# Behind three post-norms: the old residual's share of the first tile is multiplied early, and the feed of the first projection is reordered

## The chip, the cores and the metric

The kernel runs on one core of a Trainium2 chip. The metric is the device time of one execution in microseconds (us). Before the change it is 1817.71 us, the median of 3 runs that lay between 1817.23 and 1820.11 us.

## What is computed

The reference is a stack of transformer-like layers in fp32 on a 1024-wide residual `x` of 512 positions. The part that matters here is the seam between two sub-layers:

```python
x = x + rms_norm(y, norm_mix_post)      # post-norm of a sub-layer's output y
h = rms_norm(x, norm_mem_pre)           # pre-norm of the next sub-layer
q = h @ w_mq                            # its first projection
```

This happens three times with a post-norm: behind the mixer (in front of the memory attention, `w_mq`), behind the memory attention (in front of the MLP, `w_up`), and behind the MLP (in front of the first projection of the second block, `ab_w_in`). Where the root of the pre-norm enters only as a factor for each position, the kernel multiplies with the not yet normed `x * gain` and scales the product afterwards.

## The kernel before

Everything is kept transposed: a tile is 128 features (partitions) by 512 positions, and `X` holds 8 such tiles. Every operand of a matmul is split into a high part in the reduced fp32 format and a low part that holds the rest, so that each product of a weight tile and an activation tile takes three matmuls of 128x128 by 128x512: high times high, high times low, low times high. `AH` and `AL` hold high and low of `x * gain`, `WH` and `WL` those of the weights (four slots; POOL splits each loaded weight unit with two instructions, L315 and L320, as soon as TensorE has done with the slot). The names of the three seams are the pair of the sub-layer that ends and the one that begins: `o1` and `m2`, `o2` and `m3`, `m3` and `b`.

At a seam the engines do this, each in its program's order, held together by semaphores:

- TensorE ends the last output units. `post_stat` adds up the squares of `y` over the partitions with a product with ones (L494, and L496 for the last tile), then `quad` computes four output tiles (banks 0 to 3) at once, one k-tile after the other: for k-tile 0 eight matmuls with `AH` (L439, L440) and four with `AL` (L443), for each further k-tile twelve in groups of three (L454, L455, L456). `stat` (L485) multiplies the sum of squares of the new `x` with ones. Behind `m3` and `b` further units of 24 matmuls follow (L406 to L408); `m2` has none, there the attention follows (L748).
- ScalarE (ACT) squares `y` and scales it by the gain (L1404, L1405; L1443, L1445 behind the MLP), forms the root (Ln L1159, Exp L1161), and then for each tile of the new `x` writes the high part (L1174) and the square (L1177), the squares into two PSUM banks in turn. At the end it forms the root of the pre-norm (L1159, L1161 again).
- VectorE (DVE) in `x_update` does for each tile: `y` times root into a PSUM bank (`scaled`, L1981), `X += ` that (L1991), the low part `x * gain - high` (`low`, L1662), and the addition of a square (`add_square`, L1985). The low part has both its tensor inputs in SBUF. In `m2` the reads of the four banks (L1685) follow, in `m3` a clearing of `Y` (L2039) and the MLP's own work on squares (L2044, L2048).

The order on VectorE is the one written out in the code, one tile ahead:

```python
for t in range(KT):
    done(v.tensor_tensor(X[:, t, :], X[:, t, :], o, ALU.add)...)
    if t >= 2: add_square(t - 1)
    if t < KT - 1: n = scaled(t + 1)
    low(q, t, gain)
add_square(KT - 1)
```

Of the kernel before, what the change touches and what calls it, by code (L numbers as in the profile page):

```python
# [57 lines left out]
def each(stages, kind, n):  # L58
# [41 lines left out]
    "ah": each(["m1", "mm", "m2", "m3", "b", "f0", "c", "f1"], "ah", 8),  # L100
# [5 lines left out]
    "al": each(["m1", "mm", "m2", "m3", "b", "f0", "c", "f1"], "al", 8),  # L106
# [59 lines left out]
UPM = [0, 1, 2, 3, 4, 5, 0, 1]  # L166
POST_T = {"m2": 4, "m3": 4, "b": 6}
# [4 lines left out]
def build(nc, xT, memT, wstream, vecs, w_f, w_gk, gk_up, pool_w, bands, ident_d, masks_bf, gla_masks, out):  # L172
    ctx = ExitStack()
    with ctx:
# [219 lines left out]
        def _(pe):  # L394
            mm = nc.tensor.matmul

            def unit(bank, h, l, n=None, slot=None, split=None, ready=None):
# [5 lines left out]
                for k in range(KT):  # L403
                    if ready:
                        ready(k)
                    mm(bank, WH[:, slot, k, :], h(k), start=(k == 0), stop=False)  # L406
                    mm(bank, WH[:, slot, k, :], l(k), start=False, stop=False)  # L407
                    last = mm(bank, WL[:, slot, k, :], h(k), start=False, stop=(k == KT - 1))  # L408
                last.then_inc(sem("unit_done"), 1)

# [81 lines left out]
            def post_stat(p):  # L492
                pe.wait_ge(sem(f"{p}_ysum"), nth(f"{p}_ysum", 7))
                mm(B[7][:], ONES[:], SUM, start=True, stop=False)  # L494
                pe.wait_ge(sem(f"{p}_ysq"), nth(f"{p}_ysq", 8))
                mm(B[7][:], ONES[:], TMP[:, 5, :], start=False, stop=True).then_inc(sem(f"{p}_ystat"), 1)  # L496

# [244 lines left out]
            post_stat("o1")  # L742
            quad(U0["mq"], B[0:4], a_high, a_low, "mq_quad", tiles_ready("m2_al"), None, tiles_ready("m2_ah"), lambda: stat("m2"))
# [24 lines left out]
            post_stat("o2")  # L768
# [14 lines left out]
            def mlp(p, name, before=None, up=UP0, xbanks=(0, 1, 2, 3, 4, 5), tail=False):  # L783
# [3 lines left out]
                def chunk(i, first, halved=False):  # L787
                    q0 = U0[name] // 4
                    if first:
                        quad(U0[name], [B[b] for b in up[0:4]], a_high, a_low, f"{p}_quad", tiles_ready(f"{p}_al"),  # L790
                             bank_read if before else None, tiles_ready(f"{p}_ah") if p == "m3" else None)
                        stat(p)
                        for j in range(4, KT):
                            if up[j] in up[:j]:
                                pe.wait_ge(sem(f"{p}_relu"), nth(f"{p}_relu", up.index(up[j]) + 1))
                            unit(B[up[j]][:], a_high, a_low, n=U0[name] + j)
# [31 lines left out]
            post_stat("m3")  # L828
            quad(U0["bq"], B[0:4], a_high, a_low, "bq_quad", tiles_ready("b_al"), None, tiles_ready("b_ah"))
            stat("b", cols=True)  # L830
            for n in range(4, 8):
                if n >= 6:
                    pe.wait_ge(sem("b_bq_read"), nth("b_bq_read", n - 5))
                unit(B[n % 6][:], a_high, a_low, n=U0["bq"] + n)
# [317 lines left out]
        def _(act):  # L1152
# [254 lines left out]

            y_out("o1", U0["out"], "mix_post",
# [4 lines left out]
            attention("mem")  # L1413
            y_out("o2", U0["mo"], "mem_post",
# [4 lines left out]
            def mlp(p, name, post=None, banks=UP0):  # L1419
# [17 lines left out]
                if post:  # L1437
                    for t in range(KT):
# [208 lines left out]
        def _(dve):  # L1647
# [11 lines left out]

            def low(p, t, gain):  # L1660
                dve.wait_ge(sem(f"{p}_ah"), nth(f"{p}_ah", t + 1))
# [314 lines left out]
            def x_update(p, q, gain):  # L1976
# [6 lines left out]
                def add_square(t):  # L1983
                    dve.wait_ge(sem(f"{q}_xsq"), nth(f"{q}_xsq", t + 1))
                    own(v.tensor_tensor(SUM, SUM, B[POST_SQ[q][t % 2]][:], ALU.add).then_inc(sem(f"{q}_sum"), 1), f"{q}_sum")  # L1985

                dve.wait_ge(sem(f"{p}y_rb"), nth(f"{p}y_rb", 1))
                n = scaled(0)
                for t in range(KT):
                    dve.wait_ge(sem("dve_step"), nth("dve_step", n))  # L1990
                    done(v.tensor_tensor(X[:, t, :], X[:, t, :], o, ALU.add).then_inc(sem(f"{p}_x"), 1), f"{p}_x")  # L1991
                    if t >= 2:
                        add_square(t - 1)
                    if t < KT - 1:
                        dve.wait_ge(sem(f"{p}_x"), nth(f"{p}_x", t + 1))
                        n = scaled(t + 1)
                    low(q, t, gain)
                add_square(KT - 1)

            y_sum("o1")  # L2000
# [6 lines left out]
            split_out("mem", 3, 0)  # L2007
            y_sum("o2")
# [29 lines left out]
            def mlp(p, name, q=None, gain=None, post=False, tail=False):  # L2038
# [24 lines left out]
                up(i)  # L2063
                for j in range(KT - 2 if tail else KT):
# [387 lines left out]
```

## Time and profile before

| what | value |
|---|---|
| median of 3 runs | 1817.71 us |
| the profiled execution: its own time | 1819.97 us |
| the profiled execution: its span | 1818.2 us |
| mean granted TensorE clock | 0.994 |
| busy: PE / weight load / DVE / ACT / POOL | 98% / 79% / 56% / 25% / 59% |

The span runs from the first instruction to the last; the execution's own time lies 1.8 us above it. All times in the rows below are counted from the start of the span. A matmul's listed duration includes its passage through the array, so that successive matmuls overlap in the listing; what one costs is the distance from one start to the next. The same holds, to a smaller degree, for ACT and DVE.

### The profile page before, as it was taken

How to read it: one execution, taken by the hardware profiler on the slowest of the kernel's cores; microseconds unless marked ns; L12 is line 12 of the kernel's file. 1: busy time of each engine (PE TensorE's matmuls, PEld its weight loads, DVE VectorE, ACT ScalarE, POOL GpSimd, SP SyncE). 2: the span in 40 equal slices, each digit the busy share in tenths (PEclk: the TensorE clock that was granted, in tenths of full speed). 3: DMA queues.
4: the chain of work that ended last, by engine and by line, in shares of the span. 5: the costliest groups of instructions: out<-in, count | busy, mean ns of one | idle time of the engine just before them, and what ended most of it. 6: DMA issues, size and time to landing. Idle time of an engine off the chain costs nothing.

```text
span 1818.2 us, 22611 instructions
## 1 busy us (share of the span) xinstructions
PE 1775.4 (98%) x8364; PEld 1437.0 (79%) x8364; DVE 1026.7 (56%) x1194; ACT 463.4 (25%) x931; POOL 1074.8 (59%) x604
## 2 busy tenths in 40 slices
PE   9998999999999998999999999999999999999997
PEld 7775677788888886767888888887887888888886
DVE  5989465744352576175635252696766562616177
ACT  5427335401010123153201010212335320202011
POOL 7593453566666665434666666675344566666672
PEclk9999999999999999999999999999999999999999
DMA  6231221233223333211333323322221233333331
GB/s 240 68 96 58 74 80 45 82 94 102 94 93 103 93 93 104 82 47 53 98 93 95 103 92 95 102 93 81 69 71 59 81 93 95 102 93 94 102 93 47
DMA packets 46591, 161.44 MB, mean 89 GB/s; under 512 B 5232, under 2 KB 7792, under 8 KB 46384
## 3 DMA queue, kind: packets, MB, share of 16 engines
q1 hardware_dynamic: 45088, 157.31, 28.3%
q10 hardware_dynamic: 1424, 3.02, 0.5%
q8 instruction: 57, 0.93, 0.2%
q14 instruction: 22, 0.18, 0.0%
HBM read 158.21 MB, written 2.10 MB: 88 GB/s over the span
## 4 chain that ended last, share of the span: by engine, by line
PE 92%; DVE 4%; ACT 2%; issue 2%; POOL 1%; DMA 0%; DVEq 0%; POOLq 0%; ACTq 0%
PE bank L406 21%; PE bank L407 21%; PE bank L408 21%; PE bank L454 3%; PE bank L455 3%; PE bank L456 3%; PE bank L474 1%; PE bank L475 1%; PE bank L476 1%; PE bank L1002 1%; PE bank L1038 1%; PE bank L1004 1%; PE bank L1003 1%; DVE bank L1773 1%; PE bank L1053 1%
## 5 line engine op out<-in xcount | busy, mean ns | idle before, releaser
L320 POOL TENSOR_TENSOR WL<-RAW,WH 128x1024 fp32r<-128x1024 f32 x291 | 740.8, 2546 | 24.3
L315 POOL TENSOR_SCALAR WH<-RAW 128x1024 fp32r<-128x1024 f32 x291 | 313.2, 1076 | 674.7 <-PE bank L408 363.7
L406 PE MATMUL bank<-AH,WH 128*128 128x512 f32 x848 | 332.6, 392 | 0.0
L408 PE MATMUL bank<-AH,WL 128*128 128x512 f32 x848 | 330.0, 389 | 0.0
L407 PE MATMUL bank<-AL,WH 128*128 128x512 f32 x848 | 330.0, 389 | 0.0
L406 PE MATMUL bank<-HH,WH 128*128 128x512 f32 x832 | 325.2, 391 | 0.0
L407 PE MATMUL bank<-HL,WH 128*128 128x512 f32 x832 | 324.0, 389 | 0.0
L408 PE MATMUL bank<-HH,WL 128*128 128x512 f32 x832 | 323.7, 389 | 0.0
L1428 ACT ACTIVATE TMP<-bank 128x512 f32<-128x512 f32 x96 | 57.3, 596 | 777.0 <-PE bank L408 739.2
L2048 DVE TENSOR_TENSOR HL<-TMP,HH 128x512 fp32r<-128x512 f32 x96 | 239.1, 2491 | 4.0 <-ACT HH L1433 0.7
L2054 DVE TENSOR_TENSOR Y<-Y,bank 128x512 f32<-128x512 f32 x72 | 49.5, 688 | 309.3 <-PE bank L408 309.3
L2044 DVE TENSOR_TENSOR TMP<-TMP 128x512 f32<-128x512 f32 x96 | 113.0, 1177 | 174.5 <-ACT TMP L1428 174.5
L406 PEld LDWEIGHTS bank<-AH,WH 128*128 128x128 f32 x848 | 159.2, 188 | 36.8 <-issue 4.0
L407 PEld LDWEIGHTS bank<-AL,WH 128*128 128x128 f32 x848 | 159.2, 188 | 33.9 <-issue 1.2
L408 PEld LDWEIGHTS bank<-AH,WL 128*128 128x128 f32 x848 | 159.2, 188 | 33.2
L406 PEld LDWEIGHTS bank<-HH,WH 128*128 128x128 f32 x832 | 156.2, 188 | 36.1 <-DVE HL L2048 3.7
L408 PEld LDWEIGHTS bank<-HH,WL 128*128 128x128 f32 x832 | 156.2, 188 | 32.8
L407 PEld LDWEIGHTS bank<-HL,WH 128*128 128x128 f32 x832 | 156.2, 188 | 31.9
L454 PE MATMUL bank<-AH,WH 128*128 128x512 f32 x208 | 81.6, 392 | 0.0
L455 PE MATMUL bank<-AL,WH 128*128 128x512 f32 x208 | 81.2, 390 | 0.0
L456 PE MATMUL bank<-AH,WL 128*128 128x512 f32 x208 | 80.9, 389 | 0.0
L1773 DVE SCALAR_TENSOR_TENSOR bank<-Y,VC,bank 128x512 f32<-128x512 f32 x100 | 68.0, 747 | 0.1
(390 smaller groups left out, 2355.5 us busy)
## 6 DMA issues: line engine op xcount, KB each, us to landing
RAW<-wstream SPq DMA_DIRECT2D x291, 512.0 KB, 3.6
out<-Y SPq DMA_DIRECT2D x8, 256.0 KB, 2.3
X<-xT SPq DMA_DIRECT2D x3, 512.0 KB, 8.5
TMP<-memT ACTq DMA_DIRECT2D x1, 1024.0 KB, 7.3
MIX<-bands ACTq DMA_DIRECT2D x1, 768.0 KB, 4.3
RAW<-wstream SPq DMA_DIRECT2D x2, 256.0 KB, 3.9
X<-xT SPq DMA_DIRECT2D x2, 256.0 KB, 4.3
BF<-masks ACTq DMA_DIRECT2D x1, 352.0 KB, 3.9
```

The costliest lines, as they stand in the source:

```text
L315: nc.gpsimd.tensor_scalar(WH[:, s, :, :].rearrange("p k n -> p (k n)"), RAW[:, s, :], 1.0, 1.0, ALU.mult, ALU.mult).then_inc(sem("w_high"), 1)
L320: nc.gpsimd.tensor_tensor(WL[:, s, :, :].rearrange("p k n -> p (k n)"), RAW[:, s, :], f32(WH[:, s, :, :].rearrange("p k n -> p (k n)")), A ...
L406: mm(bank, WH[:, slot, k, :], h(k), start=(k == 0), stop=False)
L407: mm(bank, WH[:, slot, k, :], l(k), start=False, stop=False)
L408: last = mm(bank, WL[:, slot, k, :], h(k), start=False, stop=(k == KT - 1))
L454: mm(banks[j][:], wh, h(k), start=(k == 0), stop=False)
L455: mm(banks[j][:], wh, l(k), start=False, stop=False)
L456: last = mm(banks[j][:], wl, h(k), start=False, stop=(k == KT - 1))
L1428: nc.scalar.activation(TMP[:, j % 4, :], B[banks[j] if first else j % 4][:], ACT.Relu).then_inc(sem(f"{p}_relu"), 1)
L1773: ins = v.scalar_tensor_tensor(out=SG[:, cc, :] if j == CONV_W - 1 else acc, in0=U[:, cc, j:j + S], scalar=w, in1=acc, op0=ALU.mult, op1=A ...
L2044: v.tensor_tensor(TMP[:, 4 + j % 2, :], TMP[:, j % 4, :], TMP[:, j % 4, :], ALU.mult).then_inc(sem(f"{p}_hsq"), 1)
L2048: v.tensor_tensor(HL[:, j, :], TMP[:, 4 + j % 2, :], f32(HH[:, j, :]), ALU.subtract).then_inc(sem(f"{p}_hlow"), 1)
```

## The change

The first k-tile of the new operand is split as old `X` plus the new addend, which is possible since the product is linear. The part of the old `X` (`x_part`, twelve matmuls into banks 0 to 3) is multiplied from `AH[7]`, `AL[7]`, written ahead of the seam (`x_high`, `x_low`), and stands directly behind (for `b` half of it ahead of) the last sum of squares of `y`. For the addend, `AH[0]` is computed by VectorE straight from `Y[0]` and the root. The tiles of `X` are then updated in the order 1, 2, 3, 0, 4 to 7. On TensorE the high parts of k-tiles 0, 1, 2 come ahead of their low parts, and from k-tile 3 on high and then low, tile by tile. ACT writes a second copy of `x * gain` into a PSUM bank (`xg`), from which VectorE subtracts the high part (`low_part`), so that this subtraction has one operand in PSUM. The squares use one bank where they used two. Behind `m3` and `b`, `AH[0]` and `AL[0]` are written again from the whole `X[0]` at the end, and the fifth unit takes k-tile 0 last.

```diff
+POST_ORDER = (1, 2, 3, 0, 4, 5, 6, 7)
+POST_XG = {"m2": 6, "m3": 6, "b": 5}
...
-            def post_stat(p):
+            def post_quad(p, q, n, done, bank_free=None, ahead=0, last_k=None):
...
+                def x_part(j):
+                    if bank_free:
+                        pe.wait_ge(sem(f"{p}_yg"), nth(f"{p}_yg", bank_free[j]))
+                    wh, wl = weights(0, j)
+                    mm(B[j][:], wh, AH[:, 7, :], start=True, stop=False)
+                    mm(B[j][:], wl, AH[:, 7, :], start=False, stop=False)
+                    return mm(B[j][:], wh, AL[:, 7, :], start=False, stop=False)
+
                 pe.wait_ge(sem(f"{p}_ysum"), nth(f"{p}_ysum", 7))
                 mm(B[7][:], ONES[:], SUM, start=True, stop=False)
...
+                for j in range(ahead):
+                    x_part(j)
                 pe.wait_ge(sem(f"{p}_ysq"), nth(f"{p}_ysq", 8))
                 mm(B[7][:], ONES[:], TMP[:, 5, :], start=False, stop=True).then_inc(sem(f"{p}_ystat"), 1)
+                for j in range(ahead, 4):
+                    last = x_part(j)
...
+                for k in range(3):
...
+                for k in range(3):
+                    pe.wait_ge(sem(f"{q}_al"), nth(f"{q}_al", k + 1))
...
+                for k in range(3, KT):
+                    pe.wait_ge(sem(f"{q}_ah"), nth(f"{q}_ah", k))
...
+                    pe.wait_ge(sem(f"{q}_al"), nth(f"{q}_al", k + 1))
+                    for j in range(4):
+                        if last_k and k == KT - 1 and j == 2:
+                            last_k()
...
-            post_stat("o1")
-            quad(U0["mq"], B[0:4], a_high, a_low, "mq_quad", tiles_ready("m2_al"), None, tiles_ready("m2_ah"), lambda: stat("m2"))
+            post_quad("o1", "m2", U0["mq"], "mq_quad", [OUT_BANKS.index(j) + 1 for j in range(4)], last_k=lambda: stat("m2"))
...
+                            post_quad("o2", p, U0[name], f"{p}_quad", (5, 6, 7, 8))
...
+            post_quad("m3", "b", U0["bq"], "bq_quad", ahead=2)
...
             def normed_post(p, gain, x_ready):

-                for t in range(KT):
-                    x_ready(t)
-                    nc.scalar.activation(AH[:, t, :], X[:, t, :], ACT.Copy, scale=vec(gain, t)).then_inc(sem(f"{p}_ah"), 1)
-                    if t >= 3:
-                        act.wait_ge(sem(f"{p}_sum"), nth(f"{p}_sum", t - 2))
-                    nc.scalar.activation(B[POST_SQ[p][t % 2]][:] if t else SUM, X[:, t, :], ACT.Square).then_inc(sem(f"{p}_xsq"), 1)
+                for n, t in enumerate(POST_ORDER):
+                    x_ready(n)
+                    if t == KT - 1:
+                        act.wait_ge(sem(f"{p}_xpart"), nth(f"{p}_xpart", 1))
+                    if t:
+                        nc.scalar.activation(AH[:, t, :], X[:, t, :], ACT.Copy, scale=vec(gain, t)).then_inc(sem(f"{p}_ah"), 1)
+                        if t > 1:
+                            act.wait_ge(sem(f"{p}_al"), nth(f"{p}_al", t))
+                        nc.scalar.activation(B[POST_XG[p]][:], X[:, t, :], ACT.Copy, scale=vec(gain, t)).then_inc(sem(f"{p}_xg"), 1)
+                    if n >= 2:
+                        act.wait_ge(sem(f"{p}_sum"), nth(f"{p}_sum", n - 1))
+                    nc.scalar.activation(B[POST_SQ[p][0]][:] if n else SUM, X[:, t, :], ACT.Square).then_inc(sem(f"{p}_xsq"), 1)
+                if p != "m2":
...
...
+                def low_part(t):
+                    dve.wait_ge(sem(f"{q}_xg"), nth(f"{q}_xg", t or KT))
+                    done(v.tensor_tensor(AL[:, t, :], B[POST_XG[q]][:], f32(AH[:, t, :]), ALU.subtract).then_inc(sem(f"{q}_al"), 1), f"{q}_al")
+
+                first = TMP[:, 0, :]
                 dve.wait_ge(sem(f"{p}y_rb"), nth(f"{p}y_rb", 1))
...
+                done(v.scalar_tensor_tensor(out=AH[:, 0, :], in0=Y[:, 0, :], scalar=vec(gain, 0), in1=B[7][:],
+                                            op0=ALU.mult, op1=ALU.mult).then_inc(sem(f"{q}_yh"), 1), f"{q}_yh")
...
+                n = scaled_by_root(1, 0)
+                added(1, n)
+                n = scaled_by_root(2, 1)
+                first_step = done(v.tensor_tensor(first, Y[:, 0, :], B[7][:], ALU.mult).then_inc(sem("dve_step"), 1), "dve_step")
+                added(2, n)
...
+                done(v.scalar_tensor_tensor(out=AL[:, 0, :], in0=first, scalar=vec(gain, 0), in1=f32(AH[:, 0, :]),
+                                            op0=ALU.mult, op1=ALU.subtract).then_inc(sem(f"{q}_al"), 1), f"{q}_al")
+                n = scaled_by_root(3, 2)
+                low_part(1)
+                added(3, n)
+                low_part(2)
+                added(0, first_step)
+                for t in range(4, KT):
+                    n = scaled_by_root(t, t - 1 if t == 4 else t)
+                    add_square(t - 3)
+                    added(t, n)
+                    low_part(t - 1)
+                add_square(5)
+                low_part(7)
+                add_square(6)
+                add_square(7)
+                if q != "m2":
+                    low_part(0)
```

## Rows read from the trace of the kernel before

**Rows 1.** The page: span.
```profile
span 1818.2 us, 22611 instructions
```

**Rows 2.** Waits of PE: who for whom, total us, times, longest.
```profile
PE bank L439 <- ACT AH L1174: 11.2, 3, 3.7
```

**Rows 3.** Chain that ended last, first seam: start us, us, what.
```profile
250.61 0.67 ACT bank L1159
...
251.98 0.71 DVE bank L1981
...
254.30 0.47 PE bank L439
...
278.95 1.29 DVE MIX L1685 x2
```

**Rows 4.** Engines by stretch: clock is the figure behind POOL.
```profile
255.80:259.10 3.30, 3.30 (x9) 2.60 (x8) 3.21 (x6) 2.19 (x4) 0.00 (x0) 0.50 0.00 0
278.70:284.20 5.50, 3.35 (x13) 1.56 (x12) 4.71 (x12) 2.01 (x8) 3.40 (x2) 1.00 0.26 81
```

**Rows 5.** Timeline, PE, end of the first seam.
```profile
276.21 0.39 PE L456 MATMUL bank<-AH,WL 128*128 128x512 f32 x1
276.44 1.02 PE L485 MATMUL bank<-TMP,ONES 128*128 128x512 f32 x2
```

**Rows 6.** Timeline, PE's stat in the second and third seam.
```profile
353.90 1.02 PE L485 MATMUL bank<-TMP,ONES 128*128 128x512 f32 x2
...
712.76 1.02 PE L485 MATMUL bank<-TMP,ONES 128*128 128x512 f32 x2
```

**Rows 7.** Timeline, DVE: `scaled` of tile 0, seams 2 and 3.
```profile
328.09 0.70 DVE L1981 TENSOR_TENSOR bank<-Y,bank 128x512 f32<-128x512 f32 x1 [4.09 <-ACT bank L1161]
...
686.98 0.70 DVE L1981 TENSOR_TENSOR bank<-Y,bank 128x512 f32<-128x512 f32 x1 [3.22 <-ACT bank L1161]
```

**Rows 8.** Timeline, ACT, first seam.
```profile
248.79 0.60 ACT L1404 ACTIVATE TMP<-bank 128x512 f32<-128x512 f32 x1 [4.26 <-PE bank L408]
249.29 0.68 ACT L1405 ACTIVATE Y<-bank,VC 128x512 f32<-128x512 f32 x1
...
253.44 0.72 ACT L1174 ACTIVATE AH<-X,VC 128x512 fp32r<-128x512 f32 x1 [1.55 <-DVE X L1991]
254.06 0.62 ACT L1177 ACTIVATE TMP<-X 128x512 f32<-128x512 f32 x1
...
256.20 0.58 ACT L1177 ACTIVATE bank<-X 128x512 f32<-128x512 f32 x1
```

**Rows 9.** Timeline, DVE, ahead of the first seam's sums.
```profile
225.62 0.43 DVE L1972 COPY TMP<-TMP 128x512 f32<-128x512 f32 x1 [11.09 <-ACT TMP L1404]
```

**Rows 10.** Timeline, DVE, first seam.
```profile
256.33 0.75 DVE L1662 SCALAR_TENSOR_TENSOR AL<-X,VC,AH 128x512 fp32r<-128x512 f32 x1
257.00 0.68 DVE L1991 TENSOR_TENSOR X<-X,bank 128x512 f32<-128x512 f32 x1
257.59 0.68 DVE L1985 TENSOR_TENSOR TMP<-TMP,bank 128x512 f32<-128x512 f32 x1
258.31 0.70 DVE L1981 TENSOR_TENSOR bank<-Y,bank 128x512 f32<-128x512 f32 x1
...
264.07 2.12 DVE L1662 SCALAR_TENSOR_TENSOR AL<-X,VC,AH 128x512 fp32r<-128x512 f32 x1
...
274.22 0.68 DVE L1985 TENSOR_TENSOR TMP<-TMP,bank 128x512 f32<-128x512 f32 x1
```

**Rows 11.** Timeline, DVE, behind the second seam.
```profile
351.92 3.47 DVE L2039 MEMSET Y<- 128x4096 f32 x1 [0.92 <-DVE TMP L1985]
...
377.39 1.12 DVE L2044 TENSOR_TENSOR TMP<-TMP 128x512 f32<-128x512 f32 x1 [1.51 <-ACT TMP L1428]
378.54 2.77 DVE L2048 TENSOR_TENSOR HL<-TMP,HH 128x512 fp32r<-128x512 f32 x1
```

**Rows 12.** Chain that ended last, the MLP's first `down` unit.
```profile
381.48 0.38 PE bank L406
```

More of the change, by code:

```diff
@@ L395, in _, with unit @@
             mm = nc.tensor.matmul
-            def unit(bank, h, l, n=None, slot=None, split=None, ready=None):
+            def unit(bank, h, l, n=None, slot=None, split=None, ready=None, order=range(KT)):
                 if n is not None:
@@ new lines, in post_quad @@
+                for k in range(3):
+                    pe.wait_ge(sem(f"{q}_al"), nth(f"{q}_al", k + 1))
+                    for j in range(4):
+                        wh, wl = weights(k, j)
+                        last = mm(B[j][:], wh, AL[:, k, :], start=False, stop=False)
+                    if k == 1:
+                        last.then_inc(sem("unit_done"), 1)
+                for k in range(3, KT):
+                    u = k // 2
+                    if k % 2 == 0:
+                        pe.wait_ge(sem(f"raw_split{u}"), nth(f"raw_split{u}", n // 4 + 1))
+                    pe.wait_ge(sem(f"{q}_ah"), nth(f"{q}_ah", k))
+                    for j in range(4):
+                        wh, wl = weights(k, j)
+                        mm(B[j][:], wh, AH[:, k, :], start=False, stop=False)
+                        mm(B[j][:], wl, AH[:, k, :], start=False, stop=False)
+                    pe.wait_ge(sem(f"{q}_al"), nth(f"{q}_al", k + 1))
+                    for j in range(4):
+                        if last_k and k == KT - 1 and j == 2:
+                            last_k()
+                        wh, wl = weights(k, j)
+                        last = mm(B[j][:], wh, AL[:, k, :], start=False, stop=(k == KT - 1))
+                        if k == KT - 1 and j < 3:
+                            last.then_inc(sem(done), 1)
+                    if k % 2 == 1:
+                        last.then_inc(sem("unit_done"), 1)
@@ L1437, in mlp @@
                 if post:
+                    x_high("b", "mix2_0")
                     for t in range(KT):
@@ L1998, in x_update @@
-                add_square(KT - 1)
+                    if t > 1:
+                        dve.wait_ge(sem(f"{q}_sum"), nth(f"{q}_sum", t - 1))
+                    done(v.tensor_tensor(SUM, SUM, B[POST_SQ[q][0]][:], ALU.add).then_inc(sem(f"{q}_sum"), 1), f"{q}_sum")
+                def low_part(t):
+                    dve.wait_ge(sem(f"{q}_xg"), nth(f"{q}_xg", t or KT))
+                    done(v.tensor_tensor(AL[:, t, :], B[POST_XG[q]][:], f32(AH[:, t, :]), ALU.subtract).then_inc(sem(f"{q}_al"), 1), f"{q}_al")
@@ new lines, in added @@
+                def added(t, step):
+                    dve.wait_ge(sem("dve_step"), nth("dve_step", step))
+                    done(v.tensor_tensor(X[:, t, :], X[:, t, :], o if t else first, ALU.add).then_inc(sem(f"{p}_x"), 1), f"{p}_x")
+                n = scaled_by_root(1, 0)
[3 more added lines that the diff above has]
+                added(2, n)
@@ L2000, in _ @@
+                added(0, first_step)
[10 more added lines that the diff above has]
+                    low_part(0)
+            x_low("m2", "mem_pre")
             y_sum("o1")
@@ L2007, in _ @@
             split_out("mem", 3, 0)
+            x_low("m3", "mlp_pre")
             y_sum("o2")
@@ L2063, in mlp @@
                 up(i)
+                if post:
+                    x_low("b", "mix2_0")
                 for j in range(KT - 2 if tail else KT):
```

75 lines of the change are left out of this document (51 added, 24 removed).

## The prediction

> **What bounds the kernel now.** The page gives the span that the sum is made against, 1818.2 us [rows 1]; the execution's own time is 1.8 us more, and that lies 2.3 us above the median of the runs, so I take differences and add them to the median of 1817.7. TensorE is listed as busy nearly throughout, so the next view is who makes it wait: the largest entry of all is the first matmul with `AH` at a seam, three times up to 3.7 us, 11.2 in all [rows 2]. The chain of the first seam shows what lies in that gap: the last sum of squares of `y` is out at 250.6, then Ln, Exp, `y` times root at 251.98, the addition, the high part, and TensorE at 254.30 [rows 3]. The stretches show a second cost: after that idle time the clock is granted at 0.50 (1.2 GHz) for 3.3 us in which TensorE works without a gap [rows 4], which costs about 1.7 us. So each seam holds at most 3.7 + 1.7 = 5.4 us to be won, 16 in all. TensorE then runs without a gap, a matmul each 0.23 us, up to `stat`, whose first matmul starts at 276.44 [rows 5]. In the first seam the chain goes from there over the root to the reads of the banks at 278.95 [rows 3], and the attention behind it waits for these; in the others `stat` stands at 353.90 and 712.76, behind all of the quad [rows 6], and units follow it at once. The root of `y` reaches VectorE in the same shape in all three, at 251.98, 328.09 and 686.98, so that the second seam is the first plus 76.11 us and the third plus 435.00 [rows 7]. In these clocks `stat` starts at 276.44, 277.79 and 277.76. What I ask is when it starts after the change.
>
> **The parts and their prices.** On TensorE, `x_part` adds 12 matmuls at each seam, 36 in all, 36 x 0.23 = 8.2 us. At the first two they follow the last sum of squares and fill 2.7 of the 3.7 idle us; at the third half of them stand ahead of it, in the gap of about 1.2 us while ACT squares the last tile. The wait for the new data ends earlier too, since `AH[0]` comes from one VectorE instruction instead of two and one on ACT. So from 250.57 on TensorE would need 12 + 96 = 108 matmuls x 0.227 = 24.5 us and be done at 275.1, if it were fed. That its gap goes I take as certain. No transfer is added to SP's queue, and POOL only learns of the free weight slots a little earlier.
>
> `x_high` and `x_low` are three instructions of 0.72 on ACT and three of 0.75 on VectorE. They stand in queues that are idle there: ACT waits 4.26 us for TensorE [rows 8], VectorE 11.09 us ahead of the first sums [rows 9]. I cost them at nothing; without that cover they would be 1.5 us a seam.
>
> The feed is what decides. For the walk I need the distances from start to start. On VectorE a two-tensor instruction lets the next start after 0.59 to 0.60 us, the three-operand one after 0.67, and one that waits for its predecessor's result after 0.72 [rows 10]. On ACT the high part of 0.72 lets the square start after 0.62, a square (0.58 to 0.60) the next after 0.50 [rows 8]. Between engines about 0.03 pass, to TensorE 0.1. The new copy `xg` from SBUF into PSUM is in no row: it is bounded by the square into PSUM at 0.58 and the copy into SBUF at 0.72; squares take 0.04 less into PSUM than into SBUF, so I take 0.68, the next instruction 0.10 before its end. The low part moves from 0.75 to the 0.68 of an instruction with a PSUM operand, and above all it no longer meets POOL: one of the old ones took 2.12 [rows 10]. That is 1.4 us a seam off VectorE's own time. Against it stand the second product for tile 0 and the added copies on ACT.
>
> Walk of the first seam, VectorE from 251.98: `AH[0]`, then 17 instructions in the written order (two of them held by their predecessor, 0.1 each, and the low part of tile 2 held 0.2 by its copy) bring it to the second `add_square` at 262.8, ending 263.5. Up to there the new order is ahead: TensorE has done k-tiles 0 to 3 at 264.2, where before it was not done with tile 3 until 266.9 (42 matmuls of 0.227 ahead of `stat` at 276.44). Now look at ACT's order. It squares each tile into the one bank left, so the square of a tile waits for the `add_square` of the one before. The square of tile 0 stands ahead of the high part of tile 4 and waits for the addition that ends at 263.5: square 263.5, high part 264.0 to 264.75, copy to 265.33. TensorE waits 0.7 us for that high part. VectorE waits for the copy, 1.35 us, as its low part of tile 4 stands ahead of its next `add_square`. This then closes into a ring, in which neither engine is busy but each waits for the other: addition 0.69 + 0.03, square 0.50, high part of the next tile 0.62, its copy 0.68 + 0.04, low part 0.60, `scaled` 0.60, next addition: 3.76 us for a tile. TensorE needs 12 x 0.227 = 2.72. Third addition at 266.56, fourth at 270.32; then no `scaled` is left, 3.15 for a round: fifth at 273.47, low part of tile 7 at 276.03, sixth addition at 276.63, square of tile 7 to 277.93, seventh addition to 278.65, `stat` at 278.75. TensorE gets the high part of tile 7 at 275.42 and would be done with the quad at 278.24, so the sum is what ends last.
>
> Compared: first seam 278.75 - 276.44 = 2.31 us late, second 278.75 - 277.79 = 0.96, third 278.75 - 277.76 = 0.99; together 4.26. What was won at the front (2.7 us at tile 3) is given back with 1.03 us a tile and with the three additions that now stand behind the last update: before, the last one started at 274.22 [rows 10], 2.2 us ahead of its use, so there was cover, and now there is none.
>
> Behind the second seam something is late too. The clearing of `Y` (3.47 us, from 351.92 on, 0.92 behind its predecessor) and the MLP's squares queue on VectorE behind the new last low part, that of tile 0, which ends at about 355.9 instead of 351.0: ACT writes high part and copy for it only behind the last square. That is 4.9 us, 3.9 more than TensorE's own lateness. VectorE idled 1.51 ahead of the last hidden tile's square, and finished that tile's low part, 378.54 plus 2.77, at 381.31; TensorE took it at 381.48, a matmul listed with 0.38 instead of 0.23, so it waited 0.15 [rows 11, 12]. So there is no slack at the very end, and of the 3.9 us between 0 and 3.9 - 1.5 = 2.4 stay. VectorE idles more than that one time, and much of its 2.77 is waiting for POOL, which shifts as well; nearer to nothing, I take 0.5. At the third seam units of 5.4 us cover the second writing of `AH[0]`; I cost it at nothing, and without cover it is about 2 us.
>
> Sum: 4.26 + 0.5 = 4.8 us slower, a span of 1823.0 and 1822.5 on the median.
>
> **Rivals.** Faster: the ring doesn't bind, and TensorE is fed as it could be. For it speaks that each engine alone has the time: VectorE 4 x 0.60 = 2.4 us a tile, ACT 1.8, TensorE 2.72. Then `stat` starts at 274.7 in the first seam (two matmuls short of the end) and at 275.1 in the others: 1.7 + 2.7 + 2.7 = 7.1 us less, 1810.6. Against it speak the two waits in the order of the diff. It turns from slower to faster when the ring, which runs three rounds a seam, takes 1.4 / 3 = 0.5 us less, at 3.3 us. No row here gives such short distances. 0.13.
>
> No difference that can be told (a measurement of this kernel tells about 0.2%, 3.6 us): the same ring but shorter. With the copy at 0.60 `stat` comes 0.4 earlier in each seam, with VectorE's distances at 0.57 about 0.6. Then the sum is +1 to +3.6, about 1820. 0.27.
>
> Slower still, by the clock: now TensorE waits about 1 us in each 3.8. A stretch with more waiting, 3.35 us busy in 5.5, was granted 1.00 [rows 4]; the halving came behind 3.7 us without any work. So I don't expect it. If a stretch of 3.3 us at 0.50 falls into each seam, 1.65 us of work are lost, of which the next wait takes up 1.0 unless it is the last tile: 0.6 to 1.7 a seam, 1824 to 1827. The Trainium skill, in TensorE: Matmul & The Clock Gate, section A second HAM failure mode: psum-queue depth-cycling, says that frequent micro-idles between groups of matmuls can make the clock swing between its two levels; by that rule this rival is the result, by the row it isn't. 0.08.
>
> The Trainium skill, in SBUF — State Buffer, section SBUF: two separate sides, says that VectorE and POOL share a port pair as an exclusive lock, which a VectorE instruction with two SBUF inputs needs; by it the new low parts never stall. The 2.12 agrees, and by the ring above it gives no time back.
>
> **How the numbers follow.** The forecast, slower by over 3.6 us through the ring, has 0.52. With the clock rival slower has 0.60, same 0.27, faster 0.13. The bounds of the copy (0.58 to 0.72, about 0.4 us a seam down and 0.2 up), of VectorE's distances (0.5 a seam down, more if a wait between engines costs 0.08 instead of 0.03, 0.5 up) and of the stage behind the second seam (0 to 2.4) give about 1819.5 to 1826; for the smaller ring I take 1818.5 to 1826.
>
> **What would show it.** Right: no idle time of 3.7 us and no stretch at 0.50 at the seams; from VectorE's first use of the root to `stat` 26.8 us in all three (24.5, 25.8 and 25.8 before); TensorE waiting for ACT's high part at tiles 4 to 7, 0.4 to 1.0 us each; VectorE waiting 1.3 to 2 us for ACT's copy at these tiles, ACT about 2 us for VectorE's addition; low parts that never exceed 0.7 us. Wrong: TensorE in one run from the root to `stat` (the ring does not bind); a clock of 0.50 behind tile 4; or a later MLP whose first `down` unit waits for more than 2.5 us.

## The result, and the profile after

The changed kernel takes 1824.51 us (median of 8 runs, 1822.19 to 1827.38), the kernel before on the same chip 1817.92 (8 runs, 1817.23 to 1821.61): a ratio of 1.0033 with a 95% interval of 1.0024 to 1.0041, so 6.6 us slower. The forecast was 4.8 slower, 1822.5 within 1818.5 to 1826. The profiled execution is the slowest of the eight, 1827.4 us at a span of 1825.5. A second profile of the same kernel (run 7 below) has a span of 1822.2; where the two differ, both are given.

To compare traces I cut each at the points the prediction used: VectorE's first use of the root (251.98, 328.09, 686.98 before [rows 3, 7]) and the first matmul of `stat` (276.44, 353.90, 712.76 before [rows 5, 6]). In us:

| stretch | before | after | after, second profile |
|---|---|---|---|
| start to root 1 | 251.98 | 250.47 | 250.32 |
| seam 1: root to `stat` | 24.46 | 26.84 | 26.86 |
| attention: `stat` 1 to root 2 | 51.65 | 53.84 | 52.35 |
| seam 2 | 25.81 | 26.86 | 26.85 |
| MLP and next front: `stat` 2 to root 3 | 333.08 | 333.52 | 333.47 |
| seam 3 | 25.78 | 26.86 | 26.85 |
| `stat` 3 to the end | 1105.44 | 1107.11 | 1105.50 |

All three seams now last 26.8 to 26.9 us. They are 2.38, 1.05 and 1.08 longer, 4.51 together. First the page's span:

```profile
span 1825.5 us, 22727 instructions
```

The waits of TensorE (for whom, total us, times, longest). The answers to [rows 2] are L536 and L552:

```profile
PE bank L552 <- ACT AH L1243: 6.5, 9, 0.8
...
PE bank L814 <- DVE MIX L1775: 2.2, 2, 1.7
...
PE bank L496 <- DVE TMP L2077: 1.1, 3, 0.7
...
PE bank L536 <- DVE AH L2085: 0.9, 1, 0.9
...
PE bank L410 <- DVE HL L2172: 0.3, 1, 0.3
```

The three waits of up to 3.7 us at the first matmul with new data are down to one listed, of 0.9. In their place stand nine waits for ACT's high part and three at `stat`, 7.6 us together. So the gap was indeed filled, and a new wait took its place. Its cause is one round of the chain that ended last, in the first seam (start us, us, what; L2077 is `add_square`, L1249 the square, L1243 the high part, L1246 the new copy, L2081 the low part, L2071 `scaled`):

```profile
261.37 0.60 DVE TMP L2077
262.01 0.04 issue
262.05 0.60 ACT bank L1249
262.65 0.64 ACT AH L1243
263.29 0.59 ACT bank L1246
263.88 0.02 issue
263.91 0.04 DVE AL L2081
263.94 0.57 issue
264.51 0.69 DVE bank L2071
265.20 0.60 DVE TMP L2077
265.82 0.60 ACT bank L1249
```

From 261.37 to 265.20, 3.8 us, the chain never touches TensorE: addition, square, high part, copy, low part, `scaled`, addition. Both engines wait in it. VectorE's timeline (in brackets the idle time before the instruction, and who ended it):

```profile
263.91 0.69 DVE L2081 TENSOR_TENSOR AL<-bank,AH 128x512 fp32r<-128x512 f32 x1 [1.35 <-ACT bank L1246]
...
267.68 0.69 DVE L2081 TENSOR_TENSOR AL<-bank,AH 128x512 fp32r<-128x512 f32 x1 [1.29 <-ACT bank L1246]
```

ACT's timeline, same stretch:

```profile
262.05 0.60 ACT L1249 ACTIVATE bank<-X 128x512 f32<-128x512 f32 x1 [1.85 <-DVE TMP L2077]
262.59 0.70 ACT L1243 ACTIVATE AH<-X,VC 128x512 fp32r<-128x512 f32 x1
263.20 0.67 ACT L1246 ACTIVATE bank<-X,VC 128x512 f32<-128x512 f32 x1
265.82 0.60 ACT L1249 ACTIVATE bank<-X 128x512 f32<-128x512 f32 x1 [1.95 <-DVE TMP L2077]
```

And TensorE's, at tiles 4 and 6, at `stat` and at the attention's first matmuls:

```profile
263.44 0.47 PE L552 MATMUL bank<-AH,WH 128*128 128x512 f32 x1 [0.62 <-ACT AH L1243]
...
270.98 0.47 PE L552 MATMUL bank<-AH,WH 128*128 128x512 f32 x1 [0.85 <-ACT AH L1243]
...
277.31 1.12 PE L496 MATMUL bank<-TMP,ONES 128*128 128x512 f32 x2 [0.69 <-DVE TMP L2077]
...
280.61 1.30 PE L814 MATMUL bank<-MIX 128*128 128x256 f32 x4 [1.69 <-DVE MIX L1775]
```

Low part to low part is 3.77 us. TensorE waits 0.62 to 0.85 us at tiles 4 to 6 (0.60 to 0.85 in the other two seams); at tile 7, where one round is 3.18, no wait is listed. `stat` is what gets its data last. What the prediction did not have is behind the last of these rows. The stretches of the changed kernel (us, busy us of PE, PEld, DVE, ACT and POOL, then the clock, DMA share and GB/s):

```profile
258.00:277.30 19.30, 16.39 (x68) 11.98 (x66) 12.77 (x21) 9.29 (x16) 10.35 (x6) 1.00 0.25 82
282.50:289.00 6.50, 6.20 (x21) 4.91 (x22) 3.48 (x13) 3.53 (x13) 0.07 (x1) 0.50 0.29 81
808.10:811.40 3.30, 3.30 (x10) 2.27 (x11) 2.91 (x7) 1.76 (x5) 0.00 (x0) 0.50 0.39 150
```

With the short waits of the ring the clock stays at 1.00 (in the other two seams too, 331 to 358 and 691 to 718.5 us), and the dip of before at 255.8 [rows 4] is gone. But the clock is at 0.50 (1.2 GHz) for 6.5 us in the attention, behind the wait of 1.69 us for the reads of the banks. The windows shown lie inside the low stretches, which are up to 0.3 us longer than they; differences of 0.1 us between windows mean nothing. In the second profile that stretch is half as long:

```profile
282.30:285.50 3.20, 2.90 (x8) 1.89 (x9) 1.99 (x8) 1.86 (x7) 0.13 (x1) 0.50 0.50 157
```

The attention's length follows the low stretch: 2.19 us more than before with 6.5 us at half clock, 0.70 more with 3.2 us. The third row above, at 808 us, lies in code that the change does not touch, and the second profile has no such stretch; the last stretch of the table is 1105.50 there, as before.

### The profile page after: what moved, and what is told of

The parts are those of the page before. It is cut to its first block, busy times and chain, and to the rows that moved or that the text cites. A ratio compares the mean times of both kernels' runs of the same rounds, so it can differ in the third digit from the quotient of the medians.

```text
span 1825.5 us, 22727 instructions
## 1 busy us (share of the span) xinstructions
PE 1785.5 (98%) x8400; PEld 1440.9 (79%) x8400; DVE 1020.2 (56%) x1202; ACT 478.5 (26%) x956; POOL 1070.4 (59%) x604
## 4 chain that ended last, share of the span: by engine, by line
PE 86%; DVE 7%; ACT 3%; issue 3%; POOL 1%; DMA 0%; DVEq 0%; POOLq 0%; ACTq 0%
PE bank L410 21%; PE bank L411 20%; PE bank L412 20%; PE bank L465 2%; PE bank L467 2%; PE bank L466 2%; PE bank L485 1%; PE bank L487 1%; PE bank L486 1%; PE bank L1068 1%; PE bank L1104 1%; DVE bank L2071 1%; DVE TMP L2077 1%; PE bank L1070 1%; PE bank L1069 1%
## 5 line engine op out<-in xcount | busy, mean ns | idle before, releaser
L410 PE MATMUL bank<-AH,WH 128*128 128x512 f32 x848 | 332.6, 392 | 0.0
L411 PE MATMUL bank<-AL,WH 128*128 128x512 f32 x848 | 330.0, 389 | 0.0
L412 PE MATMUL bank<-AH,WL 128*128 128x512 f32 x848 | 330.0, 389 | 0.0
L2168 DVE TENSOR_TENSOR TMP<-TMP 128x512 f32<-128x512 f32 x96 | 108.6, 1131 | 173.3 <-ACT TMP L1512 173.2
L1517 ACT ACTIVATE HH<-TMP 128x512 fp32r<-128x512 f32 x96 | 61.1, 636 | 3.0
L465 PE MATMUL bank<-AH,WH 128*128 128x512 f32 x124 | 48.4, 390 | 0.0
L467 PE MATMUL bank<-AH,WL 128*128 128x512 f32 x124 | 48.3, 389 | 0.0
```

The costliest lines, as they stand in the source:

```text
L410: mm(bank, WH[:, slot, k, :], h(k), start=(i == 0), stop=False)
L465: mm(banks[j][:], wh, h(k), start=(k == 0), stop=False)
L467: last = mm(banks[j][:], wl, h(k), start=False, stop=(k == KT - 1))
L1517: nc.scalar.activation(HH[:, j, :], TMP[:, j % 4, :], ACT.Square).then_inc(sem(f"{p}_hhigh"), 1)
L2168: v.tensor_tensor(TMP[:, 4 + j % 2, :], TMP[:, j % 4, :], TMP[:, j % 4, :], ALU.mult).then_inc(sem(f"{p}_hsq"), 1)
```

## The experiments

Unless said otherwise each edit is made to the changed kernel. Ratios are against the kernel before on the same chip, which took 1818.56 us there in experiments 1 to 4 and 1818.89 in 5 to 8 (medians of 21 runs each).

**1. The square one tile later.** The ring theory names one place at which ACT meets VectorE too early: the square of a tile stands ahead of the next tile's high part and copy. Here it stands behind them.

```diff
+def square(n):
+    if n >= 2:
+        act.wait_ge(sem(f"{p}_sum"), nth(f"{p}_sum", n - 1))
+    nc.scalar.activation(B[POST_SQ[p][0]][:] if n else SUM, X[:, POST_ORDER[n], :], ACT.Square).then_inc(...)
 ...    # per tile: high part, copy xg, then
-                    if n >= 2:
-                        act.wait_ge(sem(f"{p}_sum"), nth(f"{p}_sum", n - 1))
-                    nc.scalar.activation(B[POST_SQ[p][0]][:] if n else SUM, X[:, t, :], ACT.Square)...
+                    if n:
+                        square(n - 1)
+                square(KT - 1)
```

> Edit: only ACT's order. The square of a tile is issued behind the high part and the copy of the next tile, still in one bank, with the same waits. Ring theory (each tile waits addition, square, high part, copy, low part, 3.76 us): the ring is cut, TensorE is fed as fast as it can go, and from VectorE's first use of the root to stat it takes 22.6 us in the first seam and 23.2 in the other two (26.8 measured after the change; 24.5, 25.8, 25.8 before). That is 1.9 + 2.6 + 2.6 = 7.1 us less than before the change: 1811, ratio 0.996. Rival, VectorE or ACT is simply overloaded by the added instructions: the order doesn't matter, 26.8 us stay, 1824. Rival, one bank for the squares is too few: stat stays within 1 us of 26.8, since the square still waits for the addition.

Measured: 1812.39 us (1808.06 to 1815.23), ratio 0.9958, 0.9947 to 0.997, so 6.2 us below the kernel before where 7.1 were expected. The seams last 22.63, 23.06 and 23.09, 7.27 less than before, and the attention 52.31, 0.66 more. ACT's and VectorE's timelines (L1241 is the square, L2086 the low part):

```profile
264.43 0.60 ACT L1241 ACTIVATE bank<-X 128x512 f32<-128x512 f32 x1 [0.49 <-DVE TMP L2082]
...
266.81 0.60 ACT L1241 ACTIVATE bank<-X 128x512 f32<-128x512 f32 x1 [0.49 <-DVE TMP L2082]
```

```profile
262.51 0.69 DVE L2086 TENSOR_TENSOR AL<-bank,AH 128x512 fp32r<-128x512 f32 x1
...
264.91 0.68 DVE L2086 TENSOR_TENSOR AL<-bank,AH 128x512 fp32r<-128x512 f32 x1
```

ACT's wait shrinks from 1.9 to 0.49, VectorE has none at tiles 4 to 6, and low parts come every 2.40 us instead of 3.77. TensorE is the bound: its `stat` follows with no wait. The attention's first matmuls still wait 1.70 us, and a low clock still follows:

```profile
275.07 1.02 PE L496 MATMUL bank<-TMP,ONES 128*128 128x512 f32 x2
...
278.26 1.29 PE L814 MATMUL bank<-MIX 128*128 128x256 f32 x4 [1.70 <-DVE MIX L1780]
```

```profile
280.30:283.60 3.30, 2.76 (x10) 1.80 (x10) 2.09 (x9) 1.86 (x7) 0.00 (x0) 0.51 0.51 159
```

No work is taken away, no bank added; only the order of one queue differs. The ring is shown, and with it what it costs: 4.21, 3.80 and 3.77 us a seam (26.84 - 22.63 and so on), 11.8 together.

**2. The low part from SBUF again.** The copy `xg` and its wait are taken out of the ring; the low part is `scalar_tensor_tensor` from `X`, as before.

```diff
-                        if t > 1:
-                            act.wait_ge(sem(f"{p}_al"), nth(f"{p}_al", t))
-                        nc.scalar.activation(B[POST_XG[p]][:], X[:, t, :], ACT.Copy, scale=vec(gain, t)).then_inc(...)
...
-                    dve.wait_ge(sem(f"{q}_xg"), nth(f"{q}_xg", t or KT))
-                    done(v.tensor_tensor(AL[:, t, :], B[POST_XG[q]][:], f32(AH[:, t, :]), ALU.subtract)...)
+                    dve.wait_ge(sem(f"{q}_ah"), nth(f"{q}_ah", t or KT))
+                    done(v.scalar_tensor_tensor(out=AL[:, t, :], in0=X[:, t, :], scalar=vec(gain, t),
+                                                in1=f32(AH[:, t, :]), op0=ALU.mult, op1=ALU.subtract)...)
```

> Edit: the second copy in PSUM is taken out, the low part is formed as before the change from X in SBUF with one three-operand instruction; the rest as after the change. Ring theory: the ring loses the copy and runs in 3.25 us a tile, root to stat 25.9, 26.1, 26.1 us, so 2.3 us less than after the change and some of the wait in the first down unit gone: 1822, provided that the low parts meet POOL at most once a seam. Rival, POOL's hold on VectorE costs more than the copy: low parts of 2.1 us sit in the ring, root to stat 27.5 or more, 1826 or more.

Measured: 1822.55 us (1819.31 to 1826.09), ratio 1.002, 1.0011 to 1.0029. The seams last 26.43, 26.42 and 26.48, some 0.4 shorter than with the copy; I had expected 25.9 to 26.1. VectorE's timeline, first seam:

```profile
263.37 1.24 DVE L2076 SCALAR_TENSOR_TENSOR AL<-X,VC,AH 128x512 fp32r<-128x512 f32 x1 [0.77 <-ACT AH L1243]
...
267.12 0.75 DVE L2076 SCALAR_TENSOR_TENSOR AL<-X,VC,AH 128x512 fp32r<-128x512 f32 x1 [0.71 <-ACT AH L1243]
...
270.38 1.55 DVE L2076 SCALAR_TENSOR_TENSOR AL<-X,VC,AH 128x512 fp32r<-128x512 f32 x1 [0.71 <-ACT AH L1243]
```

VectorE's wait in the ring goes from 1.3 to 0.7, 2.3 us less over the four tiles of a seam. But four of the low parts in seam 1 now take 1.01, 1.24, 1.55 and 0.89 instead of 0.75 and eat 1.7 of it, and each costs 0.07 more besides, being a three-operand instruction. Each of the four ends 0.53 to 0.55 us behind the end of the POOL instruction that runs when it starts, as the third of these rows does behind this one:

```profile
270.35 1.05 POOL L319 TENSOR_SCALAR WH<-RAW 128x1024 fp32r<-128x1024 f32 x1 [3.48 <-PE bank L559]
```

The second, with POOL idle, takes 0.75. With an operand in PSUM none of the seven in seam 1 takes over 0.69. So the copy and the PSUM operand are nearly an even trade: without them the ring is still there.

**3. Without old X's part.** What fills the gap is taken away: the kernel leaves out old `X`'s share of the first tile, 36 matmuls, so that its first product is not whole.

```diff
                 def x_part(j):
                     if bank_free:
                         pe.wait_ge(sem(f"{p}_yg"), nth(f"{p}_yg", bank_free[j]))
-                    wh, wl = weights(0, j)
-                    mm(B[j][:], wh, AH[:, 7, :], start=True, stop=False)
-                    mm(B[j][:], wl, AH[:, 7, :], start=False, stop=False)
-                    return mm(B[j][:], wh, AL[:, 7, :], start=False, stop=False)
...    # and the semaphore behind them with its wait; k-tile 0 opens the banks
```

> Edit: the 12 matmuls of the old X's part are left out at each seam (so the old X's share of the first tile is missing from the three projections); all else as after the change. Ring theory: TensorE has slack from tile 4 on, so the 36 matmuls cost nothing and save nothing; root to stat stays at 26.8 us and the time at 1824, even though the idle time of some 2.3 us at the front and perhaps a stretch at half clock come back. Rival, the added TensorE work is the loss: 36 x 0.23 = 8 us less, 1816.

Measured: 1824.99 us (1822.85 to 1825.93), ratio 1.0031, 1.0019 to 1.0043; the seams last 26.85, 26.85 and 26.84, as in the changed kernel. Its waits of TensorE, and a stretch:

```profile
PE bank L531 <- DVE AH L2078: 6.9, 3, 2.3
PE bank L547 <- ACT AH L1236: 3.4, 6, 0.8
```

```profile
252.50:255.70 3.20, 3.20 (x9) 2.46 (x9) 3.17 (x6) 2.58 (x4) 0.00 (x0) 0.50 0.39 147
```

The idle gap is back (three times 2.3) and so is the low clock behind it, and neither moves `stat` by more than 0.02. Under the ring, the 36 matmuls cost nothing and bought nothing.

**4. Matmuls in the waits around the first `stat`.** To cover TensorE's waits around the first `stat`, one matmul whose result no one uses goes ahead of `stat`, two behind the quad, in seam 1 only.

```diff
+            def stat_covered():
+                mm(B[4][:], ONES[:], X[:, 1, :], start=True, stop=True)
+                stat("m2")
+            post_quad("o1", "m2", ..., last_k=stat_covered)
+            for _ in range(2):
+                mm(B[4][:], ONES[:], X[:, 1, :], start=True, stop=True)
```

> Edit: three matmuls with ones into a bank that nobody reads (0.86 us each) are added in the first seam alone, one ahead of stat while TensorE waits for the sum of squares, two behind the quad while it waits for the reads of the banks; the result is untouched. In the profile after the change the clock was granted at 0.50 for 6.8 us in the attention, which began 2 us behind this wait, and not before the change, where six matmuls of the quad stood behind stat. Theory: TensorE's idle time around stat (0.7 + 1.7 us) brings the low clock in the attention, in most runs; with it covered the attention runs at 1.00 and the time falls by 1.5 to 2.5 us, to 1822.5. Rival, the low clock comes from the attention itself or at random: no change, 1824.5. If the added matmuls delay something: up to 1 us more.

Measured: 1824.38 us (1820.58 to 1825.55), ratio 1.0027, 1.0016 to 1.0038. A stretch of its profile, and the attention is 51.72 us long:

```profile
278.00:292.00 14.00, 12.59 (x74) 9.04 (x74) 10.68 (x35) 8.39 (x30) 1.80 (x1) 1.00 0.13 37
```

The profile says what the theory says: clock 1.00, and 0.63 and 2.12 us less than the changed kernel's two attentions. The times don't confirm it: 1822.5 was expected, the median is where the rival had it, and the intervals overlap. The profiled execution is the fastest of the seven, 3.8 us below their median; 2.6 us of its lead over the changed kernel's second profile lie ahead of the first root. The mean clocks of the seven executions lean towards the theory: 0.995 to 0.997, median 0.996, against 0.993 to 0.997, median 0.995, in the changed kernel's twelve (a stretch of 3.4 us at 0.50 takes 0.001 off the mean).

**5. One bank for the squares, in the kernel before.** An edit to the kernel before, which has two banks in turn.

```diff
-                    if t >= 3:
-                        act.wait_ge(sem(f"{p}_sum"), nth(f"{p}_sum", t - 2))
-                    nc.scalar.activation(B[POST_SQ[p][t % 2]][:] if t else SUM, X[:, t, :], ACT.Square)...
+                    if t >= 2:
+                        act.wait_ge(sem(f"{p}_sum"), nth(f"{p}_sum", t - 1))
+                    nc.scalar.activation(B[POST_SQ[p][0]][:] if t else SUM, X[:, t, :], ACT.Square)...
```

> Edit of the kernel before the change: the squares go into one bank instead of two in turn, and each waits for the addition of the one before; nothing else. Ring theory: in the old order no low part stands between an addition and the next one's square except as VectorE's own work, and the high part follows the update, not the square, so one bank alone closes no ring: each square comes some 0.6 us later, the last addition of 2.2 us cover loses about 0.7, root to stat stays 24.5, 25.8, 25.8 us and the time within 1 us of before, 1818.5. Rival, the single bank is the cause: stat later by 1 to 2.4 us a seam, 1822 or more.

Measured: 1817.81 us (1816.11 to 1820.23), ratio 0.9994, 0.9985 to 1.0003. The second and third seams last 25.79 and 25.74 (25.81 and 25.78 before). The first lasts 25.45, 0.99 more, but not through the bank: its low clock lasted twice as long as the 3.3 us of [rows 4].

```profile
250.00:256.60 6.60, 5.64 (x13) 4.45 (x14) 6.38 (x11) 3.67 (x6) 0.00 (x0) 0.50 0.28 79
```

One bank alone does no harm. It takes the new order too: with `low_part(t - 1)` ahead of `add_square`, the addition that frees the bank waits for ACT, which waits for the bank. Whether two banks in the new order would also cut the ring was not run.

**6. Experiment 1, with the waits around the first `stat` shortened.** The square one tile later, `stat` ahead of all four of the last low-part matmuls instead of two, and one extra matmul behind the quad in seam 1.

```diff
-                        if last_k and k == KT - 1 and j == 2:
+                        if last_k and k == KT - 1 and j == 0:
...
             post_quad("o1", "m2", ...)
+            mm(B[4][:], ONES[:], X[:, 1, :], start=True, stop=True)
```

> Edit: the later squares of the second run (root to stat 22.6, 23.1, 23.1 us), and in the first seam stat ahead of all four low-part matmuls of k-tile 7 instead of ahead of the last two, and one matmul with ones into a bank that nobody reads behind the quad, so that TensorE waits about 0.7 instead of 1.7 us for the reads. Expected by the ring and the clock theory: root to stat 22.2 in the first seam, attention and what follows up to the next root 51.7 instead of 52.3 to 53.8 us, so 0.4 + 0.6 to 2 us less than with the later squares alone: 1811. Rival, the low clock in the attention does not hang on this wait: 1812.

Measured: 1809.55 us (1809.26 to 1812.31), ratio 0.9957, 0.9944 to 0.9971. The seams last 22.19, 23.07 and 23.07, the attention 51.64. TensorE's timeline around `stat`, and the stretch:

```profile
271.69 1.02 PE L496 MATMUL bank<-TMP,ONES 128*128 128x512 f32 x2
272.14 1.49 PE L559 MATMUL bank<-AL,WH 128*128 128x512 f32 x4
273.48 1.02 PE L810 MATMUL bank<-X,ONES 128*128 128x512 f32 x2
274.87 1.30 PE L815 MATMUL bank<-MIX 128*128 128x256 f32 x4 [0.38 <-DVE MIX L1781]
```

```profile
272.00:282.00 10.00, 8.27 (x37) 4.67 (x35) 6.43 (x18) 4.86 (x15) 3.41 (x2) 1.00 0.36 105
```

The attention's first matmuls wait 0.38 instead of 1.69, the clock stays at 1.00. It has the lowest median of all kernels here and beats both the kernel before and the changed one. From run 1 (ratio 0.9958), whose attention still lasts 52.31, the times do not tell it apart; the profiles do, by 0.44 in the seam and 0.67 in the attention.

**7. The changed kernel once more.** No edit: a second profile, since the first is of the slowest execution.

> The changed kernel itself, for a second profile. Ring theory: root to stat 26.8, 26.9, 26.9 us to 0.1, as in the first. Clock theory: from stat to the next root 51.7 us plus 0.7 or 2.1, depending on how long the low clock lasts in the attention; the stretch ahead of the first seam, which the change does not touch, differs by up to 3 us between profiles of any kernel here and is part of the spread of the times, 1824.5. Rival: the excess over the ring's price comes from the seams themselves, whose stretches then differ from the first profile's.

Measured: 1825.2 us (1823.97 to 1826.52), ratio 1.0039, 1.0024 to 1.0055. Its stretches stand in the table, its low clock in the last row ahead of the experiments. Seams and MLP repeat within 0.05 us, so ring and queue belong to the kernel. The length of the low clock does not repeat, and the one at 808 us is absent.

**8. Experiment 1 without old X's part.** With the ring cut, is the filled gap worth anything? The kernel leaves out old `X`'s share of the first tile, as in experiment 3; both edits are shown there and under 1.

> Edit: the later squares, and the 12 matmuls of the old X's part left out (the old X's share of the first tile is missing from the three projections). With the ring cut TensorE sets the end of the seam, so here the filled gap can be priced. By count alone: 12 matmuls fewer, but TensorE waits 2.3 us for the root's product, root to stat 22.5 and 23.1 us, the same as with them; then filling the gap by itself buys nothing, time 1812.4. Clock theory: the idle time brings a stretch at 0.50 back within the quad (as it stood in the profile of the third run), 1.0 to 1.7 us a seam: root to stat 23.6 to 24.2 and 24.1 to 24.8, 1816.

Measured: 1816.36 us (1815.17 to 1818.18), ratio 0.9987, 0.9978 to 0.9997. Run 1 has 0.9947 to 0.997, so this kernel is slower although 36 matmuls are fewer. The seams last 22.62, 24.23 and 24.36, against 22.63, 23.06 and 23.09 there. A stretch of the first seam and one of the second:

```profile
253.00:256.00 3.00, 3.00 (x13) 2.22 (x13) 2.93 (x6) 1.40 (x3) 0.00 (x0) 1.00 0.54 175
...
327.30:330.60 3.30, 2.97 (x7) 2.44 (x8) 3.23 (x6) 1.30 (x2) 0.00 (x0) 0.50 0.55 164
```

Filling the gap is worth 1.2 and 1.3 us in the second and third seam, through the clock. In the first there was no low clock in this execution, although TensorE waited as long there as in run 3 (2.32 in both), and the seam is as long without the filling as with it: 12 fewer matmuls pay for the idle time. This execution is not typical: its mean clock is 0.994, and eight of the ten have 0.991 or 0.992, so most had more low clock than it shows. So the new head of the seam is worth having, but only once the ring is gone.

## Why the forecast was right, step by step

**The ring** was the term that decided, and it held: 4.26 forecast, 4.51 measured. The walk put the second `add_square` 10.8 us behind the root (10.81 measured, 261.28 - 250.47), the seventh 25.98 behind it (26.10, from 250.47 to 276.57), `stat` 26.77 (26.84). A round was to be 3.76 and is 3.77 from low part to low part; the copy, which no row of before showed, was set at 0.68 and takes 0.67. The rows that were asked of it are there but for one: TensorE waits 0.60 to 0.85 at tiles 4 to 6, but has no listed wait at tile 7, where 0.4 or more was expected; VectorE waits 1.29 to 1.89, ACT 1.85 to 1.95 in the full rounds and 1.35 in the last two. Run 1 cuts the ring by order alone and gets 22.63, 23.06 and 23.09; that is what the prediction's faster rival worked out for a TensorE that is fed (274.7 - 251.98 = 22.7, and 23.1). The rival's sum for the seams was right, and its condition, that the ring doesn't bind, was not met.

**The gap that goes** was right, and worth nothing under the ring (run 3). K-tiles 0 to 3 are done 12.2 us behind the root, as forecast, 14.9 before; these 2.7 us are given back from tile 4 on, where forecast.

**The low parts** with an operand in PSUM never exceed 0.69 us (the first of a seam, still from two inputs in SBUF, takes 0.75). The Trainium skill, in SBUF — State Buffer, section SBUF: two separate sides, has VectorE and POOL share a port pair that a VectorE instruction with two SBUF inputs needs; run 2 agrees, with 1.24 and 1.55 us with two SBUF inputs while POOL runs, 0.75 while it is idle, and 0.69 with one input in PSUM.

**The queue behind the second seam** was forecast at 0.5 and is 0.44 (0.39 in the second profile). VectorE's timeline of the changed kernel:

```profile
359.98 3.47 DVE L2163 MEMSET Y<- 128x4096 f32 x1 [0.80 <-issue]
...
383.15 2.77 DVE L2172 TENSOR_TENSOR HL<-TMP,HH 128x512 fp32r<-128x512 f32 x1
```

From the root of the seam the clearing starts 28.83 us on (359.98 - 331.15), before 23.83 (351.92 - 328.09): 5.0 late, 4.9 forecast. The last hidden tile's low part is 4.61 later than before [rows 11] and `stat` 4.11 later, so 0.5 arrives; TensorE waits 0.3 for it, 0.15 before. In run 6, with the ring gone, the stretch from `stat` 2 to root 3 is 332.93. The second writing behind the third seam cost nothing, as forecast: the last stretch is 1105.50 in the second profile, 1105.44 before.

**The clock** is the term that was mis-sized. The prediction gave it nothing, and its rival put it in the quad, at 0.6 to 1.7 us a seam. In the quad the granted clock is 1.00 through all of the short waits, so there the row on which I relied [rows 4] decided rightly, and against the rule that the Trainium skill gives in TensorE: Matmul & The Clock Gate, section A second HAM failure mode: psum-queue depth-cycling. The step that was off is what stands behind `stat` in the first seam, which the prediction did not walk. From `stat` to the attention's first matmul the sum, the root and the reads of the banks pass, 3.26 us before and 3.30 after. Before, six matmuls of the quad stood behind `stat` and left a wait of 0.84:

```profile
279.70 1.29 PE L748 MATMUL bank<-MIX 128*128 128x256 f32 x4 [0.84 <-DVE MIX L1685]
```

In the new order of the last k-tile only two stand there, and the wait is 1.69. That is the order's doing and not the ring's: in runs 1 and 8 `stat` has no wait at all, the wait for the reads is 1.70 and 1.69, and the low clock is there. In all six profiles with this wait (changed kernel twice, runs 1, 2, 3, 8) a low clock follows in the attention, of 3.4 us in four and of 6.8 in two; in the four without it (before, run 5: 0.84; run 6: 0.38; run 4: none) the attention runs at 1.00. It costs 0.6 to 0.7 us, or 1.9 to 2.2, against the attention of 51.65 before. The other wait, 0.69 ahead of `stat`, comes from the ring and is not needed for it. One of the prediction's signs of being wrong, a clock of 0.50 behind tile 4, thus did appear, though behind the quad and not in it. That rule may speak of this place; no run here tells. What runs 4 and 6 show is that with matmuls in the waits their two profiles have no low clock here.

**The sum.** Spans: 1825.5 - 1818.2 = 7.3 = seams 4.51, MLP 0.44, attention 2.19, the stretch at 808 us 1.67, less 1.51 by which this execution reached its first root earlier. The last two are not the change's: the stretch ahead of the first root, to which the change adds only `x_high` and `x_low` in idle time, lasts between 247.7 and 252.4 us in the ten profiles, and the stretch at 808 us doesn't repeat. With the second profile's attention the change's own part is 4.51 + 0.44 + 0.70 = 5.7, with the first's 7.1; the medians say 6.6. The 1.8 us by which the forecast fell short are of the size of the clock term, which the medians alone cannot confirm.

**What stays open:** why the low clock in the attention lasts about twice as long in one execution as in another of the same kernel, and why run 8 shows none in its first seam behind the same 2.32 us that brought it in run 3. The 2.4 us that run 8's seams are longer than run 1's are about half of what the ratios differ by; the rest may be the low clock that most of run 8's executions had and its profile lacks, but no profile shows it.

## What to carry to other kernels

When two in-order engines feed each other, walk their queues against each other, one round from an instruction to its next instance, and compare that round with what the fed engine needs; busy shares say nothing of it (VectorE had 2.4 us of work in a round of 3.77). A buffer that goes from two copies to one is safe only if the instruction that frees it does not stand behind one that waits for the engine that fills it; if it does, move the filling behind the next tile's work before asking for a bank. And filling an idle gap pays only when the engine is the bound behind it: the same 36 matmuls were worth nothing with the ring, and 1.2 us and more in each of two seams without it. Last, when the order of a stage's last tile changes, count what still stands behind the result that the next stage waits for: here four matmuls fewer doubled a wait, and the clock fell behind it.

## What the runs showed of the hardware that was not expected

- The low clock is not a fixed price. In the first seam, behind 3.7 us of idle time, it lasted 3.3 us (before) or 6.6 (run 5); behind 2.32 us, 3.2 (run 3) or nothing (run 8); in the attention, behind a wait of 1.69 us, 6.5 or 3.2 us in two executions of one kernel.
- One wait of 1.69 or 1.70 us was followed by a low clock in six profiles of six, one of 0.84 us or less in none of four. Ahead of the attention's next matmuls shorter waits follow in both cases (0.50 us).
- Waits of 0.62 to 0.85 us in each 3.8 us, through 19.3 us with 16.39 busy, left the clock at 1.00.
- A VectorE instruction of 0.75 us with two SBUF inputs took up to 2.12 us when POOL was running, and ended 0.53 to 0.55 us behind the POOL instruction's end (four in seam 1 of run 2, four in that of the kernel before).
- The stretch up to the first root, nearly the same code in all kernels here, took 247.7 to 252.4 us from profile to profile. A difference of one or two us between two single profiles is read from stretches, not from the span.
